# Who scales the softmax probabilities in the even layer, and where the reciprocal of their sums stands

## What is computed

```python
def dsa_attention(q, k, v, qi, ki, wi):
    ...
        logits = jnp.einsum('bqhd,bqnhd->bhqn', qb, kg).astype(jnp.float32) * (dh ** -0.5)
        logits = jnp.where(valid[:, None], logits, -jnp.inf)
        prob = jax.nn.softmax(logits, axis=-1)
        return jnp.einsum('bhqn,bqnhd->bqhd', prob.astype(vg.dtype), vg)
```

## Time and profile before

| | |
|---|---|
| median of 3 runs | 2313.08 us (2307.76 to 2314.1) |
| the profiled execution: its time | 2319.11 us |
| its span in the profile | 2317.8 us |
| TensorE busy | 1908.9 us (82%) |
| VectorE busy | 929.3 us (40%) |
| ScalarE busy | 685.4 us (30%) |
| mean granted clock of TensorE | 0.924 of 2.4 GHz |
| HBM traffic | 603.54 MB read, 261 GB/s over the span |

### The profile page before, as it was taken

The page is one execution under the profiler, slowest core; times in us unless marked ns, Lnnn a source line. Parts: engine busy times, 40 slices in busy tenths (PEclk is TensorE's granted clock), DMA queues, the critical chain, the costliest instruction groups (busy, mean ns, idle before and its releaser), DMA issues.

```text
span 2317.8 us, 30196 instructions
## 1 busy us (share of the span) xinstructions
PE 1908.9 (82%) x13320; PEld 1378.0 (59%) x13320; DVE 929.3 (40%) x1596; ACT 685.4 (30%) x1090; POOL 4.1 (0%) x11
## 2 busy tenths in 40 slices
PE   7799999888898999788989888888777866666656
PEld 5489999868777999766773333333255733232323
DVE  5766665657665665755341101111065501010101
ACT  4345544553524444444331000000044310000000
POOL 0000000000000000000000000000000000000000
PEclk9999999899998999989989999999988988787888
DMA  6664445441467435401048999999912499999997
GB/s 246 230 245 165 182 162 186 153 181 38 182 248 275 172 136 203 164 28 73 37 182 360 427 428 429 428 428 427 429 49 109 182 383 427 428 427 428 428 427 336
DMA packets 44787, 606.54 MB, mean 262 GB/s; under 512 B 5104, under 2 KB 5232, under 8 KB 6768
## 3 DMA queue, kind: packets, MB, share of 16 engines
q1 hardware_dynamic: 43488, 597.61, 63.3%
q0 software_dynamic: 880, 4.98, 0.6%
q10 hardware_dynamic: 288, 2.02, 0.2%
HBM read 603.54 MB, written 1.05 MB: 261 GB/s over the span
## 4 chain that ended last, share of the span: by engine, by line
PE 53%; DMA 27%; DVE 12%; ACT 6%; issue 2%; SPq 0%; DVEq 0%; ACTq 0%
PE ps L86 51%; DMA m_last_slot<-moe_down 16%; DMA m_more<-moe_up 10%; DVE m_WL L95 2%; ACT m_WH L92 1%; ACT m_mix_sc L92 1%; DVE m_od_low L101 1%; PE ps L89 1%; DMA m_ring<-ev_in 1%; DVE m_misc L104 1%; DVE m_wk L95 1%; ACT L92 1%; DVE m_ev L95 1%; DVE m_mix_sc L95 1%; DVE m_xT L95 0%
## 5 line engine op out<-in xcount | busy, mean ns | idle before, releaser
L86 PE MATMUL ps<-m_ring,m_moe_sc 128*32 128x256 f32 (+1 forms) x2304 | 415.1, 544 | 78.6 <-DMA m_ring<-moe_gate 73.5
L95 DVE TENSOR_TENSOR m_WL<-m_ring,m_WH 128x1024 fp32r<-128x1024 f32 (+1 forms) x277 | 329.9, 1202 | 269.9 <-ACT m_WH L92 269.1
L92 ACT ACTIVATE m_WH<-m_ring 128x1024 fp32r<-128x1024 f32 (+1 forms) x277 | 282.4, 1034 | 136.0 <-PE ps L86 123.7
L86 PEld LDWEIGHTS ps<-m_ring,m_moe_sc 128*32 128x32 f32 (+1 forms) x2304 | 154.4, 143 | 230.6 <-issue 121.9
L86 PE MATMUL ps<-m_more,m_moe_sc 128*32 128x256 f32 (+1 forms) x768 | 208.3, 556 | 83.6 <-DMA m_more<-moe_up 83.6
L86 PE MATMUL ps<-m_nH,m_WH 128*128 128x256 f32 x936 | 236.7, 289 | 19.5 <-ACT m_WH L92 19.5
L86 PE MATMUL ps<-m_nL,m_WH 128*128 128x256 f32 x936 | 236.4, 289 | 8.8 <-DVE m_nL L101 8.7
L95 DVE TENSOR_TENSOR m_nT<-ps,m_nT 128x512 f32<-128x512 f32 (+1 forms) x32 | 17.8, 558 | 548.1 <-PE ps L86 548.1
L86 PE MATMUL ps<-m_last_slot,m_nT 128*32 128x256 f32 (+1 forms) x768 | 186.3, 498 | 31.0 <-DMA m_last_slot<-moe_down 31.0
L92 ACT ACTIVATE m_nT<-ps 128x512 f32<-128x512 f32 (+1 forms) x64 | 31.4, 491 | 604.7 <-PE ps L89 310.5
L86 PE MATMUL ps<-m_more,m_nT 128*32 128x256 f32 (+1 forms) x768 | 189.3, 499 | 19.1 <-ACT m_nT L92 19.1
(11 more groups left out here) (299 smaller groups left out, 3023.1 us busy)
## 6 DMA issues: line engine op xcount, KB each, us to landing
m_ring<-moe_gate SPq DMA_DIRECT2D x64, 2048.0 KB, 19.1
m_ring<-moe_up SPq DMA_DIRECT2D x32, 2048.0 KB, 17.6
m_more<-moe_up SPq DMA_DIRECT2D x32, 2048.0 KB, 22.1
m_more<-moe_down SPq DMA_DIRECT2D x32, 2048.0 KB, 18.7
m_last_slot<-moe_down SPq DMA_DIRECT2D x32, 2048.0 KB, 23.2
m_ring<-ada SPq DMA_DIRECT2D x24, 2048.0 KB, 7.5
m_ring<-ffn_down SPq DMA_DIRECT2D x16, 1408.0 KB, 5.9
m_ring<-ffn_gate SPq DMA_DIRECT2D x10, 2048.0 KB, 7.6
```

The lines of the kernel that those rows point to most:

```text
L86: return Issued() if self.dry else self.e.matmul(out, lhsT, rhs, start=start, stop=stop, skip_group_check=skip)
L92: return Issued() if self.dry else self.e.activation(*a, **k)
L95: return Issued() if self.dry else self.e.tensor_tensor(*a)
```

## The change

VectorE's four multiplications by the reciprocal go; ScalarE does them as four `Copy` activations with a scale taken from `m_misc` (a new function `shares`). The reciprocal leaves `weights(i)` and stands one background step later, behind the loop's first `fill(1)`. In ScalarE's order `shares(i)` stands behind the same `fill(1)`, ahead of the exponentials of the next pair.

```diff
@@ act_even
+            def shares(i):
+                act.wait_ge(*at(("exp sum", i)))
+                for j in range(2):
+                    for t in range(2):
+                        pr, c = eP[i % 2][:, 384 * j + cut[t].start:384 * j + cut[t].stop], 4 + 2 * j + t
+                        act.activation(pr, pr, ACT.Copy, scale=e_soft[i % 2][:, c:c + 1]).then_inc(*A.mark(("prob", i)))
+
...
             for i in range(4):
                 act_jobs.fill(1)
+                shares(i)
                 if i < 3:
                     weights(i + 1)
                     act_jobs.fill(1)
@@ dve_even
                 dve.wait_ge(*V.now()).tensor_scalar(sv[:, 0:4], sv[:, 0:4], -1.0, None, ALU.mult).then_inc(*V.mark(("maxima", i)))
-                dve.wait_ge(*at(("exp", i))).reciprocal(sv[:, 4:8], sv[:, 4:8]).then_inc(*V.mark())
-                dve.wait_ge(*V.now())
-                for j in range(2):
-                    for t in range(2):
-                        c = 4 + 2 * j + t
-                        dve.tensor_scalar(pr(j, t), pr(j, t), sv[:, c:c + 1], None, ALU.mult).then_inc(*V.mark(("prob", i)))
...
             for i in range(4):
                 dve_jobs.fill(1)
+                sums = e_soft[i % 2][:, 4:8]
+                dve.wait_ge(*at(("exp", i))).reciprocal(sums, sums).then_inc(*V.mark(("exp sum", i)))
                 if i < 3:
                     weights(i + 1)
                     dve_jobs.fill(1)
```

## The result

The changed kernel takes 2320.15 us (median of 11 runs, 2317.78 to 2326.35); the kernel before, run beside it, 2314.1 us (11 runs, 2307.41 to 2322.13). The ratio is 1.0033 with a 95% interval of 1.0022 to 1.0045, so 5.1 to 10.4 us slower, middle 7.6. 2320.6 was forecast, and 7.5 us of difference. The profiled execution has a span of 2325.1 us, where the one of before had 2317.8, 7.3 us less.

A forecast was written before the change was run, and what follows sets the result against it. TensorE was taken as the bound: half the chain, and alone on it from 147.01 us. Pairs 0 to 2 at 0, pair 3's stall 5.1 and low clock 2.4 gave +7.5 on the 2313.1 median: 2320.6 us, range 2314 to 2325.

The forecast's parts named there:

- Pair 0, cost 0: Pair 0's transposes: later weights merge two TensorE gaps into one of some 6 us; cost 0, bounds -1 and +1.
- Pairs 1 and 2, hidden: Transposes of pairs 1 and 2: weights ready before TensorE asks, with 1.3 and 1.8 us to spare; cost 0.
- Pair 3, stall 5.1 us: Pair 3's transposes: late reciprocal, then scalings, make TensorE wait from 146.84 to 151.9; 5.1 us, bounds 4.8 and 5.5.
- The low clock, +2.4 us: TensorE behind pair 3's stall: runs at about half clock for a while; 2.4 us (2.36), bounds 0 and 3.4.
- The multiplications: Even layer's softmax: four multiplications taking 1.01 us on VectorE become 1.5 us on ScalarE, bounds 1.4 and 1.8.
- The sum: Whole kernel: 0 + 0 + 0 + 5.1 + 2.4 = +7.5 us, giving 2320.6 us; chance 0.60.
- Rival 1: Pair 3: the stall comes but TensorE's clock cost doesn't; 2313.1 + 5.1 = 2318.2 us, chance 0.14.
- Rival 2: Pairs 0 and 3 both cost, with longer low clock and a late pair 1; +10.3 us, 2323.4, chance 0.12.
- Rival 3: After pair 3: a later wait, such as for a DMA, swallows the delays; 2313 to 2315 us, chance 0.07.
- Rival 4: All four pairs: VectorE is the late engine, so relieving it makes the kernel faster; 2309.0 us, chance 0.07.

The follow-up runs named there:

- The first experiment: The changed kernel with pair 3's reciprocal alone moved back behind its maxima; 2317.42 us, ratio 1.0012 to the kernel before.
- the last kernel: Kernel before, with copies of pairs 0 to 2 ahead of the next exponentials, ScalarE scaling (pairs 0 and 3 earlier), reciprocals behind maxima; 2309.39 us, ratio 0.9983.

## Why the prediction was right, point by point

**Pair 0, cost 0.** Right. Pair 2's logits came 0.3 us later, counted from the load's issue, against bounds of -1 and +1. The transposes started at 116.31, 5.2 us after ScalarE's high parts began at 111.10; the prediction had 115.5 and 5.2. The unit at 111.43 was used up as cover, and the single gap was 7.41 us. The prediction said some 6, though its own starts, 108.53 and 115.5, give 7.0. The low clock behind it cost 2.15 us where 2.36 had been taken. Scalings: 1.49 us for four, forecast 1.5.

**Pairs 1 and 2, hidden.** Right; there is no idle time before their transposes.

**Pair 3, stall 5.1 us.** Right in size: 4.98. The path that it followed, VectorE's order up to the reciprocal and then the scalings, is the one in the chain above. What the prediction did not see is that ScalarE's own order made half of it. It asked when the reciprocal would be ready, found it late, and never asked when `shares(3)` would have run had the reciprocal been on time. The first experiment, written by the same reasoning, expected the gap to vanish and met 2.42 us. That the stall's size came out is therefore no proof that the wait was understood: the second delay was the shorter one and stayed hidden.

**The low clock, +2.4 us.** The mis-sized term: 1.2 us in the profiled execution, inside the bounds of 0 and 3.4. With the measured size the loop's difference is 5.0 + 1.2 + 0.3 = 6.5 us, and 6.7 were read; the 0.3 us come with the later load and not with the change. The page "TensorE: Matmul & The Clock Gate" of the Trainium skill, section "What's actually happening" in its Part 1, warns against fitting a model to a particular count of slow matmuls. The runs agree that the size is hard to tell beforehand: behind pair 3's gap it was 0 to 2.4 us in five executions. Leaving the term out would have given 5.1 us, the lower end of the measured interval.

**The multiplications.** That VectorE's 1.0 us become ScalarE's 1.5 us was right and mattered little. The page "ScalarE: Activation LUTs" of the Trainium skill, section "Rules for kernel authors", tells to leave `mul` to VectorE. The work itself agrees, 1.01 against 1.49 us; but at the late place VectorE made pair 3's gap 0.5 us shorter and opened two others of 0.95 and 0.48 us, as its order is the one that feeds the next exponentials.

**The sum.** 2320.6 against 2320.15, difference 7.5 against 7.6 in the middle of the interval. That it is so close is luck. The interval reaches from 5.1 to 10.4, the difference of the two medians is 6.05, and the loop shows 6.7 with a low clock at half the price that the sum gave it. The forecast's lower bound, 5.1 + 0 - 1, was also put too high by its own terms, since the stall's was 4.8.

**The rivals.** Rival 1 (stall without the clock) had the stall right, but the clock did fall, to 0.52 of full speed for 2.9 us. A gap without it was seen only in the first experiment, at 2.42 us. Its 5.1 us lie at the edge of the measured interval, so the time alone wouldn't have refuted it. Rival 2 (both places) fell with pair 0, which cost nothing. Rival 3 (swallowed later) is refuted by the traces: 7.07 us at pair 3's values, 7.3 at the end of the span. Rival 4 (faster, by VectorE's relief) is refuted by the result. Its mechanism exists but is small: it is the 0.8 us that the last kernel gained behind pair 2's values.

## What to carry to other kernels

In kernels whose engines run a fixed order each, price a moved instruction by what stands ahead of it in its new queue, at each repetition apart: here three of four were free and the fourth met the long background step of `zh`. When a chain passes two engines, ask for each of them when its part would have run if the other were on time; undoing the later cause alone brings back only the difference. And a gap that the profile puts down to one instruction may be held by another: here the copies in ScalarE's queue behind the next pair's exponentials, and taking these ahead was worth 5.9 us in the loop, nearly what the change cost (6.7).

## What the runs showed of the hardware

The same gap of TensorE brought the low clock in one profiled execution and not in another. With pair 3's reciprocal early it was 2.42 us, and transposes to values then took 150.81 - 147.16 = 3.65 us with the clock at full; with all reciprocals early it was again 2.42 us, and they took 147.06 - 141.92 = 5.14:

```profile
147.20:150.60 3.40, 3.40 (x30) 3.40 (x30) 1.81 (x2) 1.82 (x3) 0.00 (x0) 1.00 0.66 280
```
```profile
142.00:145.40 3.40, 3.40 (x22) 3.40 (x23) 1.81 (x2) 1.81 (x3) 0.00 (x0) 0.69 0.66 280
145.40:147.00 1.60, 1.60 (x10) 1.52 (x8) 0.15 (x1) 0.00 (x0) 0.00 (x0) 0.59 0.00 0
```

The first window is of the one kernel, the other two of the other (columns as in the earlier trace rows). A gap of some 2.4 us was thus worth 2.4 or 3.9 us; gaps of 3.84, 4.50 and 4.98 us cost 1.4, 2.4 and 1.2 us on top of themselves, and the last kernel's 1.84 us brought the low clock where 2.03 and 2.38 us did not. So the price did not follow the gap's length in these executions, and one execution of a kernel can't tell it.
